# Layer norm folded into the next product of a two-layer decoder step

## The chip, the cores and the metric

The kernel runs on one core of a Trainium2 chip. The time is the device time of one execution in microseconds (us). Three executions were timed, and their median is the time before. The times of instructions come from one more execution, taken with the hardware profiler.

The engines of the core are named TensorE (PE in the profile, its weight loads PEld), VectorE (DVE), ScalarE (ACT), GpSimd (POOL) and SyncE (SP). Each works through its own queue in order. They wait for each other with semaphores.

## The reference

264 tokens (256 of a prompt, 8 of running samples) with 2048 features go through two layers. Each layer is a mixer and an MLP, and each of the four steps ends in a layer norm of a residual sum:

```python
def layer_norm(x, g, b):
    mu = jnp.mean(xf, axis=-1, keepdims=True)
    var = jnp.mean(jnp.square(xf - mu), axis=-1, keepdims=True)
    y = (xf - mu) * lax.rsqrt(var + LN_EPS)
    return y * g + b
...
x = layer_norm(ALPHA * x + mixer(x))
x = layer_norm(ALPHA * x + jnp.square(jax.nn.relu(x @ w1)) @ w2)
```

The first layer's mixer is a sparse attention beside a convolution, the second's a pooling beside a gated MLP ("odd" in the code). Both have one input projection and one output projection. The MLP has 8192 hidden features. All is float32, and the matmuls must come close to float32.

## The kernel before

**Products.** Features lie on partitions, tokens on columns: `x`, `yacc` and `sq` are 128 x 16 x 264, with 16 tiles k of 128 features. All large products are cut into 89 weight groups `G` of 512 output features (4 banks of `psa`) by 2048 input features: 0 to 9 the first input projection, 10 to 13 its output projection (`G_EOUT`), 14 to 45 the first MLP, 46 to 52 the odd input projection (`G_OIN`), 53 to 56 the odd output projection, 57 to 88 the second MLP. An MLP is four rounds of eight groups: four "hidden" groups that give 2048 hidden features, and four "product" groups that add to `yacc`.

**Split in two.** Every product is made of three: the weights are split into `whi` (rounded to the matmul's format) and `wlo` (the rest), the input likewise into `xhi` and `xlo` (`hhi` and `hlo` for the hidden features), and L414 to L416 do high x high, high x low and low x high. A group has four pieces `p` of 4 tiles k, each with 4 banks, and so 192 matmuls of 264 columns. `split(G, p)` stands in two queues: on ScalarE (L946) it makes `whi` once the buffer is free, on VectorE (L1320) it then makes `wlo`. There are two buffers, so the split of piece 0 of the next group waits for piece 2 of this one, that of piece 1 for the end of this group, that of piece 2 for piece 0 of its own group, and that of piece 3 for piece 1. TensorE waits with `lo_ready` for each piece. The weights come by DMA a whole group ahead.

**Order.** The queues are written out by hand. In a hidden group (`hidden`), ScalarE's queue holds the splits of pieces 2 and 3 of this group (`later`), that of piece 0 of the next, then for each bank a Relu out of `psa` (L1233, which frees the bank) and the high part `hhi` of the square (L1238), and near the end the split of piece 1 of the next group. VectorE's queue holds the same splits, then the squares (L1835) and the low parts (L1838). In the first round ScalarE also makes the residual ALPHA * x (L1179).

**The norm.** `last_groups` (VectorE) and `norm` (ScalarE, TensorE) close each of the four steps. VectorE adds the product groups to `yacc` and sums them over k. In the last group it subtracts a preliminary mean of the first 12 tiles (L1765, after one matmul with ones, L843), ScalarE squares, and after the last bank TensorE sums over partitions with four matmuls with ones (L849 to L854). VectorE then makes mean, variance and inverse root, centres and divides `yacc` in five chunks (L1815, L1816), ScalarE applies gain and bias to give `x` (L1213) and its high part `xhi` (L1217), and VectorE the low part (L1811), which lets TensorE start the next group piece by piece. `L` counts the norms, 0 to 3; 0 to 2 are followed by a product, 3 by the output.

**The odd projection.** ScalarE evicts its groups straight from `psa`: group 46 into `pext` and `psx`, with a wait for all seven small loads of this layer (`odd_in`), the others through Gelu (L1277, L1287).

Of the kernel before, what the change touches and what calls it, by code (L numbers as in the profile page):

```python
# [25 lines left out]
D = 2048  # L26
# [46 lines left out]
ln_sum ln_mean ln_cent ln_sq ln_var ln_tot ln_part ln_norm ln_x ln_xhi y_init  # L73
# [4 lines left out]
win_out odd_in pin_done u_done gelu_v vtr vcopied vn_done wst_done mix_mm mix_ev pool_d pool_mm sgs_tr sgs_done  # L78
# [4 lines left out]
def build(nc, io):  # L83
    with ExitStack() as ctx:
# [32 lines left out]
        xhi = new("xhi", [128, KT, NT], F32R)  # L117
        xlo = new("xlo", [128, KT, NT], F32R)
# [45 lines left out]
        b = Region(region_b, region_a)  # L164
# [92 lines left out]
        def _(sp):  # L257
# [68 lines left out]
            for i in range(4):  # L326
                sp.wait_ge(s.ln_x, 3 * KT + 4 * i + 4)
                sp.dma_start(io.o_x[:, 4 * i * NT:(4 * i + 4) * NT], x[:, 4 * i:4 * i + 4, :].rearrange("p k t -> p (k t)"))\
                    .then_inc(s.x_out, 16)
# [4 lines left out]
        def _(pool):  # L334
# [43 lines left out]
            pool.dma_start(psx[:].rearrange("p c b w -> p (c b w)"), io.stpool).then_inc(s.odd_in, 16)  # L378
# [6 lines left out]
            pool.wait_ge(s.bank_free, 4 * (G_OIN + 1))  # L385
# [10 lines left out]
        def _(pe):  # L396
            mm = nc.tensor.matmul

            def group(G, hi, lo, xbase=None, hooks=None):

                nt = tiles(G)
                for p in range(4):
# [3 lines left out]
                    for n in range(nt):  # L406
                        if p == 0 and not (isinstance(G, int) and G == 0):
                            pe.wait_ge(s.bank_free, 4 * G - 3 + n)
                        for kk in range(4):
# [3 lines left out]
                            out = psa[:, n, 0:NT]  # L413
                            mm(out, wh, hi[:, k, :], start=(k == 0), stop=False)  # L414
                            mm(out, wh, lo[:, k, :], start=False, stop=False)  # L415
                            last = mm(out, wl, hi[:, k, :], start=False, stop=(k == KT - 1))  # L416
# [421 lines left out]
            def mean_hook(L):  # L838

                def hook(p, n):  # L840
                    if p == 0 and n == 3:
                        pe.wait_ge(s.ln_sum, L + 1)
                        mm(psm[:, 0, 0:NT], ones, s1[:], start=True, stop=True).then_inc(s.ln_mean, 1)  # L843
                return hook

            def norm(L):

                pe.wait_ge(s.ln_part, L + 1)
                mm(psm[:, 0, 0:NT], ones, s1[:], start=True, stop=False)  # L849
                mm(psm[:, 1, 0:NT], ones, s2[:], start=True, stop=False)  # L850
                pe.wait_ge(s.bank_free, 4 * (G_MLP0, G_OIN, G_MLP1, G_END)[L])
                mm(psm[:, 0, 0:NT], ones, yacc[:, KT - 1, :], start=False, stop=True)
                pe.wait_ge(s.ln_sq, 7 * L + 7)
                mm(psm[:, 1, 0:NT], ones, sq[:, KT - 1, :], start=False, stop=True).then_inc(s.ln_tot, 1)  # L854

            def mlp(G0, L, xbase, hbase):
                with pe.Fori(0, 3) as f:
                    with pe.Fori(0, 4) as g:
                        group(G0 + f * 8 + g, xhi, xlo, (s.x_ready, xbase))
# [3 lines left out]
                with pe.Fori(0, 4) as g:  # L863
                    group(G0 + 24 + g, xhi, xlo)
                group(G0 + 28, hhi, hlo, (s.hid_ready, hbase + 48))
                with pe.Fori(5, 7) as g:
# [1222 lines left out]
```

## Time and profile before

| | |
|---|---|
| median of 3 runs | 2646.7 us |
| lowest and highest | 2639.17 and 2647.37 us |
| the profiled execution | 2640.75 us |
| its span, first to last instruction | 2639.1 us |
| granted TensorE clock over the span | 0.944 of full |
| TensorE busy, matmuls | 2441.2 us, 93% |
| VectorE busy | 1472.7 us, 56% |
| ScalarE busy | 991.0 us, 38% |
| DMA | 516 MB, 196 GB/s |

A difference of two times is set against the profiled execution's own time. The share of busy time says how much an engine works over the whole span, and not whether its work is in time: an engine that is half idle can hold up another one, if what the other one wants stands late in its queue. A wait is put down to the operation that ended last before it. The granted clock is the share of its full 2.4 GHz at which TensorE was let run; 0.50 is 1.2 GHz.

### The profile page before, as it was taken

The page shows a single profiled execution, that of the slowest core. Times are in us where ns is not written, and L with a number is a line of the kernel's source. Part 1 is how long each engine was busy: PE and PEld are TensorE (multiplying, and loading weights), DVE is VectorE, ACT ScalarE, POOL GpSimd, SP SyncE. Part 2 cuts the span into 40 slices and gives each one's busy share as a digit, 9 for nine tenths or more (in the row PEclk, how much of TensorE's full clock was granted, in tenths as well). Part 3 has the DMA queues.
Part 4 walks back from the last instruction along what each step waited for, and adds up shares of the span by engine and source line. Part 5 has one row for each costly group of instructions (what it writes and reads, how often), then busy time and mean ns, then how long its engine had stood idle before and what let it go on. Part 6 is the DMA issues. An engine that isn't in the chain of part 4 may idle for free.

```text
span 2639.1 us, 51324 instructions
## 1 busy us (share of the span) xinstructions
PE 2441.2 (93%) x20534; PEld 2279.2 (86%) x20534; DVE 1472.7 (56%) x1695; ACT 991.0 (38%) x1117; POOL 87.0 (3%) x169
## 2 busy tenths in 40 slices
PE   4999998888979999999999799679899999999996
PEld 3778871577979999999999799569799999999996
DVE  3677777556665454445455644666654544444556
ACT  2233330344354344343343444233543443443433
POOL 0000013230000000000000000000000000000000
PEclk8999995888989999999999899879899999999998
DMA  7788779787535555555544354324355455455451
GB/s 284 256 311 311 267 196 267 249 262 262 177 136 200 209 199 203 186 204 200 208 181 176 128 203 175 128 77 176 113 182 183 175 182 183 175 182 184 175 182 75
DMA packets 99715, 515.98 MB, mean 196 GB/s; under 512 B 12824, under 2 KB 21048, under 8 KB 52512
## 3 DMA queue, kind: packets, MB, share of 16 engines
q1 hardware_dynamic: 88992, 467.90, 50.2%
q0 software_dynamic: 10624, 46.72, 5.4%
q8 instruction: 67, 1.10, 0.2%
q14 instruction: 32, 0.26, 0.0%
HBM read 508.17 MB, written 18.95 MB: 200 GB/s over the span
## 4 chain that ended last, share of the span: by engine, by line
PE 83%; DVE 8%; DMA 3%; ACT 2%; issue 2%; SPq 0%; POOL 0%; POOLq 0%; ACTq 0%; DVEq 0%
PE psa L414 25%; PE psa L415 24%; PE psa L416 24%; DVE wlo L1320 2%; DMA page<-in_cmp 2%; PE psa L577 2%; PE psm L450 1%; ACT whi L946 1%; PE psm L770 1%; PE psa L749 1%; DMA kbuf<-in_selk 1%; DVE yacc L1815 1%; PE psm L602 1%; DVE page L1336 1%; PE psa L602 1%
## 5 line engine op out<-in xcount | busy, mean ns | idle before, releaser
L1320 DVE TENSOR_TENSOR wlo<-wraw,whi 128x2048 fp32r<-128x2048 f32 x356 | 816.2, 2293 | 934.6 <-ACT whi L946 934.4
L414 PE MATMUL psa<-xhi,whi 128*128 128x264 f32 x3632 | 1050.4, 289 | 57.8 <-DVE xlo L1811 23.3
L946 ACT ACTIVATE whi<-wraw 128x2048 fp32r<-128x2048 f32 x356 | 681.5, 1914 | 1116.3 <-PE psa L416 1114.9
L415 PE MATMUL psa<-xlo,whi 128*128 128x264 f32 x3632 | 1041.0, 287 | 0.0
L416 PE MATMUL psa<-xhi,wlo 128*128 128x264 f32 x3632 | 1036.3, 285 | 0.0
L414 PEld LDWEIGHTS psa<-xhi,whi 128*128 128x128 f32 x3632 | 692.4, 191 | 95.0 <-issue 84.4
L415 PEld LDWEIGHTS psa<-xlo,whi 128*128 128x128 f32 x3632 | 692.5, 191 | 0.1
L416 PEld LDWEIGHTS psa<-xhi,wlo 128*128 128x128 f32 x3632 | 690.9, 190 | 0.0
L414 PE MATMUL psa<-hhi,whi 128*128 128x264 f32 x2048 | 582.6, 284 | 0.0
L415 PE MATMUL psa<-hlo,whi 128*128 128x264 f32 x2048 | 582.1, 284 | 0.0
L416 PE MATMUL psa<-hhi,wlo 128*128 128x264 f32 x2048 | 580.1, 283 | 0.0
L414 PEld LDWEIGHTS psa<-hhi,whi 128*128 128x128 f32 x2048 | 385.4, 188 | 0.1
L415 PEld LDWEIGHTS psa<-hlo,whi 128*128 128x128 f32 x2048 | 385.4, 188 | 0.1
L416 PEld LDWEIGHTS psa<-hhi,wlo 128*128 128x128 f32 x2048 | 384.8, 188 | 0.0
L1336 DVE TENSOR_TENSOR page<-page,pe_rep 128x768 f32<-128x768 f32 x128 | 115.8, 953 | 18.1 <-DMA page<-in_cmp 17.5
L450 PE MATMUL psm<-page,const 128*32 128x384 f32 x512 | 57.2, 520 | 23.3 <-DVE page L1336 23.3
L577 PE MATMUL psa<-kbuf,qzr 96*32 96x512 f32 x320 | 64.6, 903 | 13.2 <-DMA kbuf<-in_selk 13.1
L1238 ACT ACTIVATE hhi<-stage 128x264 f32 x128 | 53.5, 418 | 45.0 <-DVE stage L1835 45.0
L1116 ACT ACTIVATE pp<-pp,hg 128x128 f32<-128x128 f32 (+1 forms) x64 | 28.4, 445 | 108.9 <-DVE hg L1607 108.9
L1732 DVE TENSOR_TENSOR yacc<-psa,yacc 128x264 f32 (+1 forms) x144 | 55.4, 427 | 23.8 <-PE psa L416 23.8
L1838 DVE TENSOR_TENSOR hlo<-stage,hhi 128x264 f32 x128 | 55.1, 430 | 13.4 <-ACT hhi L1238 12.2
L1233 ACT ACTIVATE stage<-psa 128x264 f32<-128x264 f32 x128 | 48.9, 382 | 27.0 <-PE psa L416 23.4
(351 smaller groups left out, 1214.2 us busy)
## 6 DMA issues: line engine op xcount, KB each, us to landing
wraw<-in_w SPq DMA_DIRECT2D x356, 1024.0 KB, 4.8
page<-in_cmp SPq DMA_DIRECT2D x128, 384.0 KB, 4.8
kbuf<-in_selk SPq DMA_DIRECT2D x64, 192.0 KB, 5.5
kbuf<-in_selk POOLq DMA_DIRECT2D x64, 192.0 KB, 5.6
vbuf<-in_selv SPq DMA_DIRECT2D x64, 192.0 KB, 3.9
vbuf<-in_selv POOLq DMA_DIRECT2D x64, 192.0 KB, 4.0
o_win<-in_win POOLq DMA_DIRECT2D x8, 1533.0 KB, 7.7
kbuf<-in_wink SPq DMA_DIRECT2D x8, 768.0 KB, 6.6
```

Source lines behind the costliest of these rows:

```text
L414: mm(out, wh, hi[:, k, :], start=(k == 0), stop=False)
L415: mm(out, wh, lo[:, k, :], start=False, stop=False)
L416: last = mm(out, wl, hi[:, k, :], start=False, stop=(k == KT - 1))
L450: last = mm(psm[c:c + 32, 2, 0:KW], C("blkz", 28 - 4 * r, 60 - 4 * r), page[:, (2 * r + q) % 8, half * KW:half * KW + KW], start=(r == 0), ...
L577: last = mm(psa[32 * g:32 * g + 32, c % 2, :], qzr[:, r, 32 * g:32 * g + 32], kbuf[:, u % 4, :, g * 128:(g + 1) * 128], start=(r == 0), st ...
L602: last = mm(bank[32 * g:32 * g + 32, d:d + HD], p_t, vbuf[:, u % 5, q, g * HD:(g + 1) * HD], start=(q == 0 and c == 0), stop=(q == 3 and ( ...
L946: A(whi[:, p % 2, :], wraw[:, p, :], ACT.Copy).then_inc(s.hi_ready, 1)
L1238: A(hhi[:, bass.ds(4 * g + n - 1, 1), :], stage[:, n - 1:n, :], ACT.Copy).then_inc(s.hh_done, 1)
L1320: V.tensor_tensor(wlo[:, p % 2, :], wraw[:, p, :], whi[:, p % 2, :].bitcast(F32), ALU.subtract).then_inc(s.lo_ready, 1)
L1336: V.tensor_tensor(v, v, bc(pe_rep[:].rearrange("p a (g d) -> p a g d", g=1), 128, 2, KVH, HD), ALU.mult)\
L1732: V.tensor_tensor(y, psa[:, n:n + 1, 0:NT], y, ALU.add).then_inc(s.bank_free, 1)
L1838: V.tensor_tensor(hlo[:, bass.ds(4 * g + n - 1, 1), :], stage[:, n - 1:n, :], hhi[:, bass.ds(4 * g + n - 1, 1), :].bitcast(F32), ALU.subtr ...
```

## The change

The norms 0 to 2 no longer stand between the sum and the next product. The product is taken of the centred sum z times the gain g, not divided by the root. With W the weights, r the inverse root and m the remaining mean of z over the features, the next layer's input is r (z - m) g + b, so

(input @ W) = r ((z g) @ W - m (g @ W)) + b @ W.

- `xhi` and `xlo` get two more columns, 264 and 265, with g and b of the features. The groups that follow a norm (32 hidden and 7 odd ones) so have matmuls of 266 columns, and the last two columns of each bank hold g @ W and b @ W.
- `fold` takes the place of `last_groups` and `norm` for norms 0 to 2. The preliminary mean is that of the first 8 tiles and comes one group earlier (TensorE's `shift_hook`, in the third of the last four groups). All four parts of `yacc` are centred in that group. In the last group the high and low parts of z g are made, and the squares. The sums over partitions are two matmuls with ones (`total_hook`) inside piece 1 of the next product's first group. The root (`spread_root`) lies in that group between the splits of pieces 2 and 3.
- The eviction moves from ScalarE to VectorE: `evict` copies the two columns into `gb`, adds m times g @ W (a `scalar_tensor_tensor` out of `psa`, which frees the bank), and multiplies by r, all three for each bank. ScalarE's Relu or Gelu reads that and adds b @ W as its bias.
- The normalised x itself is still needed, for the residual sum. `whole` makes it in the first four groups after each of these norms: two VectorE operations over 1056 columns and four ScalarE operations for each group. In the MLPs they write `yacc`, already times ALPHA (`alph`).
- The small loads of the odd layer: `psx` has its own semaphore, and the six others are issued after x is complete and awaited later.
- Norm 3 keeps the old form (`final_groups`).

```diff
-                            out = psa[:, n, 0:NT]
-                            mm(out, wh, hi[:, k, :], start=(k == 0), stop=False)
+                            out = psa[:, n, 0:w]
+                            mm(out, wh, hi[:, k, 0:w], start=(k == 0), stop=False)
...
+            def total_hook(L):
+
+                def hook(p, n):
+                    if p == 1 and n == 1:
+                        pe.wait_ge(s.z_part, L + 1)
+                        mm(psm[:, 0, 0:NT], ones, s1[:], start=True, stop=True)
+                        mm(psm[:, 1, 0:NT], ones, s2[:], start=True, stop=True).then_inc(s.z_tot, 1)
+                return hook
...
ScalarE
+            def whole(L, i, dst, done):
+
+                act.wait_ge(s.z_norm, 4 * L + i + 1)
+                for k in range(4 * i, 4 * i + 4):
+                    ins = A(dst[:, k, :], yacc[:, k, :], ACT.Identity, scale=alph[:, 32 * L + k:32 * L + k + 1],
+                            bias=alph[:, 32 * L + 16 + k:32 * L + 17 + k])
...
+            def hidden(G, g, m, hb, first=None):
+
+                if first is not None and first[1] == 0:
+                    spread_root(first[0], G)
+                else:
                     later(G)
+                split(G + 1, 0)
+                for n in range(5):
+                    if n == 3:
+                        split(G + 1, 1)
+                    if n < 4:
+                        act.wait_ge(s.ev_done, hb + (28 if hb > 64 else 0) + 4 * m + n)
+                        A(stage[:, n, :], stage[:, n, :], ACT.Relu, bias=gb[:, n, 1:2]).then_inc(s.relu_done, 1)
+                    if n >= 1:
+                        act.wait_ge(s.sq_done, hb - 1 + 4 * m + n)
+                        A(hhi[:, bass.ds(4 * g + n - 1, 1), :], stage[:, n - 1:n, :], ACT.Copy).then_inc(s.hh_done, 1)
+                if first is not None:
+                    whole(first[0], first[1], yacc, s.y_init)
...
VectorE
+            def spread_root(L, Gn):
+
+                split(Gn, 2)
+                dve.wait_ge(s.z_tot, L + 1)
+                step(V.tensor_scalar(mean[:], psm[:, 0, 0:NT], -1.0 / D, None, ALU.mult))
...
+                inverse_root(V.tensor_scalar(rstd[:], rstd[:], EPS, None, ALU.add), rstd[:])
+                split(Gn, 3)
+
+            def evict(G, n, count):
+
+                dve.wait_ge(s.bank_done, 4 * G + n + 1)
+                V.tensor_copy(gb[:, n, :], psa[:, n, NT:NT + 2]).then_inc(s.gb_done, 1)
+                dve.wait_ge(s.gb_done, count)
+                V.scalar_tensor_tensor(stage[:, n, :], mean[:], gb[:, n, 0:1], psa[:, n, 0:NT], ALU.mult, ALU.add).then_inc(s.bank_free, 1)
+                dve.wait_ge(s.bank_free, 4 * G + n + 1)
+                V.tensor_tensor(stage[:, n, :], stage[:, n, :], rstd[:], ALU.mult).then_inc(s.ev_done, 1)
+
+            def whole(L, i):
+
+                v = yacc[:, 4 * i:4 * i + 4, :]
+                step(V.tensor_tensor(v, v, along(mean, 4), ALU.add))
+                V.tensor_tensor(v, v, along(rstd, 4), ALU.mult).then_inc(s.z_norm, 1)
...
+            def hidden(G, g, m, hb, first=None):
...
+                split(G + 1, 0)
+                dve.wait_ge(s.hid_ready, hb + 4 * m)
+                for n in range(6):
+                    if n == 4:
                         split(G + 1, 1)
+                    if n < 4:
+                        evict(G, n, hb + (28 if hb > 64 else 0) + 4 * m + n)
+                    if 1 <= n < 5:
+                        dve.wait_ge(s.relu_done, hb - 1 + 4 * m + n)
+                        V.tensor_tensor(stage[:, n - 1, :], stage[:, n - 1, :], stage[:, n - 1, :], ALU.mult).then_inc(s.sq_done, 1)
+                    if n >= 2:
+                        dve.wait_ge(s.hh_done, hb - 2 + 4 * m + n)
+                        V.tensor_tensor(hlo[:, bass.ds(4 * g + n - 2, 1), :], stage[:, n - 2:n - 1, :],
+                                        hhi[:, bass.ds(4 * g + n - 2, 1), :].bitcast(F32), ALU.subtract).then_inc(s.hid_ready, 1)
+                if first is not None:
+                    whole(*first)
```

The groups of the odd projection run the same way with Gelu and without squares: ScalarE has its split of piece 1 ahead of the fourth Gelu, VectorE behind the four evictions, and `whole` closes the first four groups in both queues.

## Rows read from the trace of the kernel before

**Rows 1.** The page, busy time, share of the span and instructions of each engine.

```profile
PE 2441.2 (93%) x20534; PEld 2279.2 (86%) x20534; DVE 1472.7 (56%) x1695; ACT 991.0 (38%) x1117; POOL 87.0 (3%) x169
```

**Rows 2.** Waits of TensorE over the span: line, releaser, us in total, times, longest.

```profile
PE psa L414 <- DVE xlo L1811: 23.3, 2, 11.7
PE psa L414 <- DVE wlo L1320: 21.2, 4, 17.4
PE psm L849 <- DVE s L1790: 18.9, 4, 5.4
PE psa L414 <- issue: 11.5, 1, 11.5
```

**Rows 3.** Windows between norms: length, busy us (x instructions) of each engine, clock, DMA.

```profile
900.00:950.00 50.00, 50.00 (x415) 50.00 (x414) 23.55 (x17) 15.75 (x9) 0.49 (x1) 1.00 0.55 209
```

**Rows 4.** Timeline of ScalarE, splits at two norms: start, duration, instruction, [idle <- releaser].

```profile
703.90 1.92 ACT L946 ACTIVATE whi<-wraw 128x2048 fp32r<-128x2048 f32 x1 [3.94 <-PE psa L416]
...
710.19 1.92 ACT L946 ACTIVATE whi<-wraw 128x2048 fp32r<-128x2048 f32 x1 [4.38 <-PE psa L416]
...
776.19 1.92 ACT L946 ACTIVATE whi<-wraw 128x2048 fp32r<-128x2048 f32 x1 [2.90 <-PE psa L416]
...
1475.05 1.92 ACT L946 ACTIVATE whi<-wraw 128x2048 fp32r<-128x2048 f32 x1 [3.94 <-PE psa L416]
...
1550.89 1.92 ACT L946 ACTIVATE whi<-wraw 128x2048 fp32r<-128x2048 f32 x1 [3.57 <-PE psa L416]
```

**Rows 5.** Timeline of VectorE in a hidden group of the first MLP.

```profile
978.34 0.77 DVE L1835 TENSOR_TENSOR stage<-stage 128x264 f32<-128x264 f32 x2
...
982.67 2.29 DVE L1320 TENSOR_TENSOR wlo<-wraw,whi 128x2048 fp32r<-128x2048 f32 x1 [1.24 <-ACT whi L946]
```

**Rows 6.** Timeline of ScalarE in the same group.

```profile
980.74 1.90 ACT L946 ACTIVATE whi<-wraw 128x2048 fp32r<-128x2048 f32 x1
...
985.83 1.92 ACT L946 ACTIVATE whi<-wraw 128x2048 fp32r<-128x2048 f32 x1 [2.88 <-PE psa L416]
```

**Rows 7.** Groups of VectorE by form: busy us, mean ns of one, idle before.

```profile
L1626 DVE TENSOR_TENSOR hg<-hg,gt 128x2 f32<-128x2 f32 x16 | 2.6, 161 | 0.6
L1518 DVE SCALAR_TENSOR_TENSOR stage<-uext,param,stage 128x256 f32<-128x256 f32 x120 | 50.9, 480 | 0.9
L1835 DVE TENSOR_TENSOR stage<-stage 128x264 f32<-128x264 f32 x128 | 52.0, 427 | 0.0
L1816 DVE TENSOR_TENSOR yacc<-yacc,rstd 128x1056 f32<-128x1056 f32 x12 | 15.1, 1259 | 1.3
```

**Rows 8.** Groups of ScalarE by form, the same columns.

```profile
L1238 ACT ACTIVATE hhi<-stage 128x264 f32 x128 | 53.5, 418 | 45.0 <-DVE stage L1835 45.0
L1213 ACT ACTIVATE x<-yacc,param 128x264 f32<-128x264 f32 x64 | 34.1, 597 | 23.3 <-DVE yacc L1816 23.3
```

**Rows 9.** Timelines: gaps of TensorE, restarts after a waited split, four x operations.

```profile
530.96 0.45 PE L624 MATMUL psm<-const,tok 128*96 128x128 f32 x1 [3.00 <-ACT ptp L1067]
...
741.91 2.11 ACT L1213 ACTIVATE x<-yacc,param 128x264 f32<-128x264 f32 x4 [1.65 <-DVE yacc L1816]
...
1543.25 0.39 PE L414 MATMUL psa<-xhi,whi 128*128 128x264 f32 x1 [1.74 <-ACT psx L1269]
...
1876.14 2.29 DVE L1320 TENSOR_TENSOR wlo<-wraw,whi 128x2048 fp32r<-128x2048 f32 x1 [0.48 <-ACT whi L946]
...
1878.48 0.39 PE L414 MATMUL psa<-xhi,whi 128*128 128x264 f32 x1 [1.41 <-DVE wlo L1320]
...
1884.58 1.92 ACT L946 ACTIVATE whi<-wraw 128x2048 fp32r<-128x2048 f32 x1 [4.58 <-PE psa L416]
```

**Rows 10.** Windows after such gaps, the columns of rows 3.

```profile
1513.70:1519.70 6.00, 5.96 (x27) 5.99 (x28) 5.89 (x5) 3.84 (x7) 0.00 (x0) 0.50 0.39 146
1543.80:1547.20 3.40, 3.40 (x18) 3.40 (x17) 1.15 (x1) 3.38 (x6) 1.27 (x2) 0.50 0.61 212
...
531.00:535.00 4.00, 4.00 (x43) 3.35 (x44) 0.00 (x0) 0.98 (x2) 0.29 (x2) 0.50 0.70 253
```

More of the change, by code:

```diff
@@ L116, in build @@
         region_b = new.next
-        xhi = new("xhi", [128, KT, NT], F32R)
-        xlo = new("xlo", [128, KT, NT], F32R)
+        xhi = new("xhi", [128, KT, NT + 2], F32R)
+        xlo = new("xlo", [128, KT, NT + 2], F32R)
+        alph = new("alph", [128, 128])
+        gb = new("gb", [128, 4, 2])
         region_a = new.next
@@ L924, in _ @@
             group(G_OOUT, xhi, xlo, (s.x_ready, 64))
-            with pe.Fori(G_OOUT + 1, G_OOUT + 3) as G:
-                group(G, xhi, xlo)
-            group(G_OOUT + 3, xhi, xlo, None, mean_hook(2))
-            norm(2)
+            group(G_OOUT + 1, xhi, xlo)
+            group(G_OOUT + 2, xhi, xlo, None, shift_hook(2))
+            group(G_OOUT + 3, xhi, xlo)
             mlp(G_MLP1, 3, 80, 65)
@@ L1185, in first_groups @@
                 for i in range(4):
-                    residual(i)
+                    residual(i, x, scale)
                 split(G0 + 1, 0)
                 split(G0 + 1, 1)
-                with act.Fori(G0 + 1, G0 + 3) as G:
-                    later(G)
-                    split(G + 1, 0)
-                    split(G + 1, 1)
-            first_groups(G_EOUT, 8)
-            def norm(L):
-                G = (G_MLP0, G_OIN, G_MLP1, G_END)[L] - 1
+                later(G0 + 1)
+                split(G0 + 2, 0)
@@ L1219, in hidden @@
[L1219 to L1238 removed]
+                        act.wait_ge(s.ln_norm, k0 + m)
@@ new lines, in hidden @@
+            def hidden(G, g, m, hb, first=None):
+                if first is not None and first[1] == 0:
+                    spread_root(first[0], G)
+                else:
+                    later(G)
+                split(G + 1, 0)
+                dve.wait_ge(s.hid_ready, hb + 4 * m)
+                for n in range(6):
+                    if n == 4:
+                        split(G + 1, 1)
+                    if n < 4:
[9 more added lines that the diff above has]
+                    whole(*first)
@@ L1841, in mlp, with products @@
             def mlp(G0, L, hb, y):
-                with dve.Fori(0, 3) as f:
-                    hidden(G0, f, hb)
+                def products(f):
                     dve.wait_ge(s.y_init, 4 * y)
```

430 lines of the change are left out of this document (263 added, 167 removed).

## The prediction, made blind

> **What bounds the kernel now.** I read the page first. TensorE is busy 93% of the span and VectorE 56% [rows 1]: the kernel is a chain of weight groups on TensorE, and the question is which waits interrupt it. The waits of TensorE give the norms: it waits for the last square sum and then for the first normalised piece of the next input, 17.1 us at each of the three inner norms (two of the long ones stand under `xlo`, the third under "issue") [rows 2]. The stretches come next: between norms TensorE is busy all 50.00 of 50 us, 415 matmuls at 120.5 ns, full clock, so nothing waits there [rows 3]. A group of 192 matmuls takes 23.3 us (the value that the split times below repeat) and a piece (a quarter) 5.83.
>
> What a norm costs in all is read from ScalarE's splits. The split of piece 2 starts when TensorE has finished piece 0 of the same group. From the last group before the norm (703.90) to the second after it (776.19) are 72.3 us, at the second norm 75.8, at the third 72.3 again (its rows repeat the first's) [rows 4]. Two undisturbed groups are 46.6, so the norms cost 25.7 + 29.2 + 25.7 = 80.6 us beyond plain groups. In them lie the waits, five small fp32 products with ones, and half clock after the idle time: from 1513.7 the granted clock is 0.50 and 27 matmuls take 6 us, 220 ns each; at full clock they would take 3.2 [rows 10].
>
> **What the change removes.** The next product starts on centred, unscaled data, so its pieces are ready before the norm's sums are, and TensorE waits for neither. I work out what remains at each inner norm. The four adds of the last group come behind a weight split and the `low` operations on VectorE, bank 0 is freed some 0.5 us late, with a restart 0.8. Two fp32 ones products inside the next group: 0.9 (one such product lengthens a piece from 5.83 to 6.29, as 703.90 to 710.19 shows for the mean product; I use 0.46 for each) [rows 4]. Root and reciprocal lie between two splits on VectorE and make pieces 2 and 3 a few tenths late each, with restarts 0.9. The mean product is moved a group earlier and not removed, 0.46. Sum 3.1, three times 9.2. Saved: 80.6 - 9.2 = **71.4 us**. The 3.6 us more of the second norm are in it: its evictions waited for the small odd-layer loads, which the change takes off ScalarE's wait. The last norm stays as it is.
>
> **The two columns.** 39 groups (32 of the two MLPs, 7 of the odd projection) x 192 matmuls get 266 columns for 264. In proportion to 120.5 ns that is 0.91 ns each, **6.8 us**. The lower bound is nothing: 264 columns take 220 ns at half clock, so 110 at full, and 120.5 is seen [rows 3, 10]; if what adds the 10.5 is not additive, the columns hide in it. I take the upper end. The Trainium skill ("TensorE: Matmul & The Clock Gate", Back-to-back issue gap) gives N/2.4 + 2.5 ns at full clock for a lone stream; this trace is 8 ns above that, and by the page two columns would be 0.83 ns, 6.2 us in all.
>
> **The eviction, the part that I think decides.** Before, ScalarE evicts a bank in one Relu. After, VectorE makes copy, multiply-add, multiply before ScalarE's Relu, then squares. The busy share says that VectorE has room (9 us in each group). The order in its queue says otherwise, because the split of piece 1 of the next group stands behind all of this, and it can't be made earlier: ScalarE's half waits for the end of the group. Take the hidden group that ends at 980.0. Before: ScalarE's half 980.74, VectorE's half 982.67 to 984.96; TensorE finishes piece 0 at 985.83 and needs it then. The spare time is 0.87 us [rows 5, 6].
>
> Now the new order, from 978.34, where VectorE leaves the preceding split [rows 5]. Durations: copy of two columns 0.17 (a two-column operation takes 0.161), multiply-add with a scalar operand 0.49 (0.480 on 256 columns), products and subtractions 0.43 [rows 7]; a dependent one follows 0.04 after the end, an independent one 0.08 before it, as the neighbours in the timeline show. Relu with a bias operand 0.54: a copy takes 0.42 and one with scale and bias 0.60 [rows 8]. Bank 0: copy 978.34, multiply-add 978.55, multiply to 979.51. Bank 1: copy 979.44, multiply to 980.61, square 0 to 980.96. Bank 2: copy 980.89, multiply to 982.06, square 1 to 982.41, low part 0 to 982.76. Bank 3: copy 982.69, multiply to 983.86, square 2, low part 1 to 984.56. ScalarE meanwhile: Relu 2 at 982.08, high part 1 to 982.97, and behind them, by its order, the split, 982.90 to 984.81. VectorE's half then runs 984.83 to 987.12, **2.16 us later than before**. TensorE stands idle for 1.3 us. A piece that starts on a waited split ends 6.14 us after the split (1878.43 to 1884.57) and not 5.83 [rows 9], so piece 1 ends at 993.3 and not 991.7: **1.6 us** a group. The banks themselves are free in time (bank 3 at 983.4, wanted at 984.4). Of the 32 hidden groups 24 are of this form: 38.4 us.
>
> On the small operations the Trainium skill ("VectorE: DVE Perf Modes", The TRN2 errata) says that each one pays a fixed latency, 120 cycles at 0.96 GHz from PSUM, and that many small tiles pay it each time; that speaks against this eviction, and its estimate for the two-column copy is 0.13 us. By it the chain would be 0.04 shorter for each bank and the sum 5 us lower.
>
> **The whole x, kept for the residual.** In the first four groups of each MLP VectorE's queue ends with square 3 and low parts 2 and 3 (to 988.38), then add and multiply over 1056 columns, 1.25 each [rows 7], to 990.86; ScalarE must wait for that, makes four with scale and bias in 2.11 [rows 9], to 992.99, and only behind them comes the split of piece 2, to 994.84, and VectorE's half to 997.15. Piece 1 was done at 993.3: idle 3.9 us, and piece 2 ends at 1003.3 for 999.1, **4.2 more**. 8 groups x (1.6 + 4.2) = 46.4 us. The residual that ScalarE made there before lay in its free time and gives nothing back.
>
> The odd projection has no squares. The same count puts the split of piece 1 at 986.42 (0.9 lost) and of piece 2 at 995.19 (idle 2.7, 2.9 lost): 4 groups x 3.8 + 2 x 0.9 = 17.0 us.
>
> **The clock after the new gaps.** After 1.74 us of idle (ended 1543.25) the next matmuls went 220 ns apart at a granted clock of 0.50, 18 of them, 1.8 us lost; after 3.00 (ended 530.96) it was 0.50; after 11.5 the loss was 2.8. After 1.41 (ended 1878.48) and the like the pace stayed full [rows 9, 10]. So I charge the 12 gaps of 2.7 to 3.9 us with 2.2 each, **26 us** (bounds 22 and 34), and the gaps of 1.3 with nothing (upper bound 1.8 for each of about 32, 58 us).
>
> **Sum**, against the profiled execution's own 2640.75 us (its span 2639.1; 6 below the median of 2646.7): -71.4 + 6.8 + 38.4 + 46.4 + 17.0 + 26 = +63.2, so **2704 us**, 2.4% slower.
>
> **Rivals.**
> (a) *The new gaps arise but the clock holds.* 2640.75 + 37 = 2678. For it: three gaps of 1.2 to 1.4 us left no trace. Against: the gap of 1.74.
> (b) *The gaps of 1.3 us lower the clock too.* 2704 plus 20 to 58, say 2735. They are just below the 1.74 that did it, and come in every group. The Trainium skill ("TensorE: Matmul & The Clock Gate", A second HAM failure mode) tells of a kernel that idled briefly between groups and kept oscillating between both clocks.
> (c) *Faster: the splits keep up.* The place is the split of piece 1 behind the evictions: up to a delay of 0.87 us it costs nothing, and I count 2.16. If the operations were some 0.3 us shorter for each bank than their rows, and the whole x fitted into the same free time, no gap would be left: 2640.75 - 71.4 + 6.8 = 2576. For it speaks only the free time by the busy shares.
> (d) *Half of it:* piece 1 keeps up and only the whole x is late: 8 x 4.2 + 4 x 2.9 = 45, clock 0 to 26: 2621 to 2647, about the same time.
>
> **How the numbers follow.** Forecast 0.50, (a) 0.20, (b) 0.13, (c) 0.08, (d) 0.09. A measurement of this kernel can tell about 0.3% (8 us) from no change. Faster: (c) and over half of (d), 0.13. Same: 0.05. Slower: 0.82. The range takes in (a) with operations 0.1 us shorter for each bank (some 20 us less over all groups) and most of (b): 2655 to 2748.
>
> **What would show it.** The timeline of a hidden group: the split of piece 1 ends 7.1 us after the group's end, TensorE waits some 1.3 us for `wlo`; in the first four groups of an MLP a second wait of about 3.9 us. Group period 24.9 and some 29 to 31 against 23.3. The waits for `wlo` (21.2 now) become by far the largest, some 90 us more; those for `xlo` and `s` vanish but for the last norm. The granted clock falls in the first groups of each MLP. The prediction is wrong if `wlo` stays near 21, or if ScalarE's split of piece 1 doesn't wait behind the Relus.

## The result, and the profile of the changed kernel

The changed kernel takes 2698.8 us (median of 4 runs, 2694.1 to 2704.5), the kernel before 2647.0 beside it (4 runs, 2639.2 to 2655.0): ratio 1.0193, 95% interval 1.0165 to 1.0221, so slower by 1.9%. The profiled execution took 2695.44 us with a span of 2693.7; that of before took 2640.75 with 2639.1. The two spans differ by 54.6 us, and this is the sum that is taken apart below.

The page's busy times, which answer to [rows 1], and the chain that ended last:

```profile
PE 2474.0 (92%) x20522; PEld 2306.7 (86%) x20522; DVE 1628.4 (60%) x2194; ACT 1003.6 (37%) x1140; POOL 86.9 (3%) x169
...
PE 68%; DVE 15%; ACT 9%; issue 5%; DMA 2%; SPq 0%; DVEq 0%; ACTq 0%; POOLq 0%; POOL 0%
```

VectorE does 156 us more work in 499 more instructions and still is busy for only 60% of the span. By that line alone nothing is wrong. The waits of TensorE (line, releaser, us in total, times, longest) say where it went:

```profile
PE psa L417 <- DVE wlo L1394: 94.8, 49, 17.5
...
PE psm L868 <- DVE s L1956: 2.6, 1, 2.6
PE psa L417 <- DVE yacc L1877: 1.7, 3, 0.6
```

Against [rows 2] the waits for `xlo` are gone and those for `s` have shrunk from 18.9 to 2.6. What is left of the three inner norms is 1.7 us in three waits of 0.5 to 0.6 for the last adds (L1877), which free the banks; the prediction had 0.5 each. In their place stands the low half of the weights: 94.8 us in 49 waits, where it was 21.2 in 4. These are the new gaps. In the first MLP, from the norm to the fifth group, and then in a later hidden group, TensorE's timeline (start, duration, instruction, [idle before <- releaser]) has them as follows:

```profile
758.70 0.39 PE L417 MATMUL psa<-xhi,whi 128*128 128x266 f32 x1 [1.34 <-DVE wlo L1394]
...
768.69 0.41 PE L417 MATMUL psa<-xhi,whi 128*128 128x266 f32 x1 [3.79 <-DVE wlo L1394]
...
789.30 0.39 PE L417 MATMUL psa<-xhi,whi 128*128 128x266 f32 x1 [1.06 <-DVE wlo L1394]
...
799.30 0.39 PE L417 MATMUL psa<-xhi,whi 128*128 128x266 f32 x1 [3.79 <-DVE wlo L1394]
...
999.55 0.39 PE L417 MATMUL psa<-xhi,whi 128*128 128x266 f32 x1 [1.05 <-DVE wlo L1394]
```

Two kinds of gap: one of about 1.05 us before piece 1 of the group that follows each hidden group, and one of 3.8 before piece 2 of the group that follows each of the first four. Why there is a gap before piece 1 stands in the timelines of VectorE and of ScalarE around the group that ends at 992.6 (the gap at 999.55 begins at 998.50, and one piece before that is 992.6). They answer to [rows 5, 6]:

```profile
993.30 0.15 DVE L1903 COPY gb<-psa 128x2 f32<-128x2 f32 x1
993.49 0.49 DVE L1905 SCALAR_TENSOR_TENSOR stage<-mean,gb,psa 128x264 f32<-128x264 f32 x1
994.02 0.43 DVE L1907 TENSOR_TENSOR stage<-stage,rstd 128x264 f32<-128x264 f32 x1
994.37 0.43 DVE L1994 TENSOR_TENSOR stage<-stage 128x264 f32<-128x264 f32 x1
994.71 0.43 DVE L1997 TENSOR_TENSOR hlo<-stage,hhi 128x264 f32 x1
995.06 0.15 DVE L1903 COPY gb<-psa 128x2 f32<-128x2 f32 x1
...
997.20 2.29 DVE L1394 TENSOR_TENSOR wlo<-wraw,whi 128x2048 fp32r<-128x2048 f32 x1 [0.32 <-ACT whi L974]
```

```profile
994.93 0.42 ACT L1309 ACTIVATE hhi<-stage 128x264 f32 x1
995.26 1.91 ACT L974 ACTIVATE whi<-wraw 128x2048 fp32r<-128x2048 f32 x1
...
1000.48 1.92 ACT L974 ACTIVATE whi<-wraw 128x2048 fp32r<-128x2048 f32 x1
...
1025.49 1.92 ACT L974 ACTIVATE whi<-wraw 128x2048 fp32r<-128x2048 f32 x1
```

VectorE works on the banks without a pause, operation after operation. ScalarE splits piece 1 only at 995.26, behind three Relus and two high parts that each wait for VectorE, and VectorE's half ends at 999.49. TensorE wanted it at 998.50. The split of piece 2 begins at 1000.48 and that of the next group at 1025.49, 25.0 us later; in the kernel before the corresponding ones, 962.54 and the 985.83 of [rows 6], are 23.29 apart.

The second kind comes from the whole x. VectorE's and ScalarE's timelines behind the third hidden group:

```profile
821.02 1.25 DVE L1912 TENSOR_TENSOR yacc<-yacc,mean 128x1056 f32<-128x1056 f32 x1
822.31 1.26 DVE L1913 TENSOR_TENSOR yacc<-yacc,rstd 128x1056 f32<-128x1056 f32 x1
827.54 4.50 DVE L1394 TENSOR_TENSOR wlo<-wraw,whi 128x2048 fp32r<-128x2048 f32 x2 [3.97 <-ACT whi L974]
```

```profile
823.60 2.10 ACT L1271 ACTIVATE yacc<-yacc,alph 128x264 f32<-128x264 f32 x4 [2.96 <-DVE yacc L1913]
825.61 3.70 ACT L974 ACTIVATE whi<-wraw 128x2048 fp32r<-128x2048 f32 x2
```

Two operations on VectorE, then four on ScalarE, then the split. VectorE itself is idle for 3.97 us ahead of its half, waiting for ScalarE's, which waited for VectorE: an engine with idle time in front of the very work that is late.

The windows of TensorE (length, busy us (x instructions) of PE, PEld, DVE, ACT, POOL, granted clock, DMA share, GB/s): 50 us of later hidden groups, and the stretch behind two of the long gaps.

```profile
955.00:1005.00 50.00, 47.90 (x386) 47.47 (x386) 31.97 (x48) 21.93 (x24) 0.49 (x1) 1.00 0.55 200
...
768.70:772.00 3.30, 3.30 (x15) 3.30 (x16) 2.14 (x1) 0.00 (x0) 0.00 (x0) 0.53 0.59 199
799.30:803.00 3.70, 3.70 (x18) 3.70 (x19) 2.15 (x1) 0.00 (x0) 0.00 (x0) 0.55 0.66 226
```

With gaps of 1.05 us in it the first window still has the full clock. Behind the gaps of 3.8 us the clock is at half: 18 matmuls in 3.70 us, which at 121.3 ns each would take 2.18, so 1.5 us are lost.

**By stretches.** I cut both traces at ScalarE's split of piece 2, as the prediction did. From the last group before the first norm to the sixth after it, before takes 165.5 us and after 171.4; over the same groups of the last norm of this kind 165.5 and 171.8; at the odd norm 169.1 and 158.9. The first four groups after each MLP norm take 30.6 (before 23.3), the first four odd groups 27.2, so the norms themselves got cheaper by 23.5 (5.9 more, of which 4 x 7.3 are these groups), 25.8 (10.2 less, in spite of 4 x 3.9) and 23.1 us, 72.4 in all. The 26 groups that follow in each MLP, of which 12 are hidden groups at 25.0, take 627.3 and 626.9 for 605.7: 21.7 and 21.2 more. The rest of the 54.6 lies in the input projection and the attention stage (3.4), in the odd layer's own mixer (4.0, with one wait in it that grew by 3.9: TensorE waits 4.4 us for the last Gelu where it waited 0.5), and in 1.2 us each at two stretches that I had not looked for: the plain output projection groups in them, with matmuls of 264 columns as before and no new operation, take 23.55 us each for 23.29.

### The profile page after: what moved, and what is told of

The parts are those of the page before. It is cut to its first block, busy times and chain, and to the rows that moved or that the text cites. A ratio compares the mean times of both kernels' runs of the same rounds, so it can differ in the third digit from the quotient of the medians.

```text
span 2693.7 us, 51259 instructions
## 1 busy us (share of the span) xinstructions
PE 2474.0 (92%) x20522; PEld 2306.7 (86%) x20522; DVE 1628.4 (60%) x2194; ACT 1003.6 (37%) x1140; POOL 86.9 (3%) x169
## 4 chain that ended last, share of the span: by engine, by line
PE 68%; DVE 15%; ACT 9%; issue 5%; DMA 2%; SPq 0%; DVEq 0%; ACTq 0%; POOLq 0%; POOL 0%
PE psa L417 20%; PE psa L418 19%; PE psa L419 19%; ACT whi L974 7%; DVE wlo L1394 5%; DVE stage L1905 2%; PE psa L580 2%; PE psm L453 2%; PE psm L773 1%; DMA kbuf<-in_selk 1%; DVE stage L1907 1%; PE psa L752 1%; DVE stage L1994 1%; DMA page<-in_cmp 1%; DVE yacc L1913 1%
## 5 line engine op out<-in xcount | busy, mean ns | idle before, releaser
L417 PE MATMUL psa<-xhi,whi 128*128 128x266 f32 (+1 forms) x3632 | 1060.0, 292 | 79.3 <-DVE wlo L1394 77.6
L418 PE MATMUL psa<-xlo,whi 128*128 128x266 f32 (+1 forms) x3632 | 1048.4, 289 | 0.0
L419 PE MATMUL psa<-xhi,wlo 128*128 128x266 f32 (+1 forms) x3632 | 1046.7, 288 | 0.0
L417 PEld LDWEIGHTS psa<-hhi,whi 128*128 128x128 f32 x2048 | 386.7, 189 | 19.3 <-DVE wlo L1394 13.6
L1306 ACT ACTIVATE stage<-stage,gb 128x264 f32<-128x264 f32 x128 | 65.5, 512 | 144.3 <-DVE stage L1907 144.3
L1905 DVE SCALAR_TENSOR_TENSOR stage<-mean,gb,psa 128x264 f32<-128x264 f32 x156 | 76.4, 490 | 5.5
L1309 ACT ACTIVATE hhi<-stage 128x264 f32 (+1 forms) x128 | 53.7, 419 | 65.9 <-DVE stage L1994 65.9
L1907 DVE TENSOR_TENSOR stage<-stage,rstd 128x264 f32<-128x264 f32 x156 | 67.5, 433 | 5.3
```

What stands on the lines that cost most here:

```text
L417: mm(out, wh, hi[:, k, 0:w], start=(k == 0), stop=False)
L418: mm(out, wh, lo[:, k, 0:w], start=False, stop=False)
L419: last = mm(out, wl, hi[:, k, 0:w], start=False, stop=(k == KT - 1))
L1306: A(stage[:, n, :], stage[:, n, :], ACT.Relu, bias=gb[:, n, 1:2]).then_inc(s.relu_done, 1)
L1905: V.scalar_tensor_tensor(stage[:, n, :], mean[:], gb[:, n, 0:1], psa[:, n, 0:NT], ALU.mult, ALU.add).then_inc(s.bank_free, 1)
L1907: V.tensor_tensor(stage[:, n, :], stage[:, n, :], rstd[:], ALU.mult).then_inc(s.ev_done, 1)
```

## The experiments

Three things are open. Does the place of the split in the queues decide, or the amount of VectorE's work? Do the short gaps cost clock? And what slows groups that do nothing new? (The texts written before the runs call runs 1, 2 and 3 e1, e2 and e3, the two of run 4 e7 and e8, run 5 e4, the three of run 6 e5, e6 and e9, and run 7 e10.)

**1. Evict first.** The same instructions as the changed kernel in another order. VectorE makes the four evictions and square 0, then its half of the split, then the other squares and the low parts; ScalarE has its half behind the first Relu (the odd groups: behind the first Gelu instead of the third).

```diff
ScalarE
-                for n in range(5):
-                    if n == 3:
-                        split(G + 1, 1)
...
+                relu(0)
+                split(G + 1, 1)
+                high(0)
+                for n in range(1, 4):
+                    relu(n)
+                for n in range(1, 4):
+                    high(n)
VectorE
-                for n in range(6):
-                    if n == 4:
-                        split(G + 1, 1)
...
+                for n in range(4):
+                    evict(G, n, hb + (28 if hb > 64 else 0) + 4 * m + n)
+                    if n == 1:
+                        square(0)
+                split(G + 1, 1)
+                for n in range(1, 4):
+                    square(n)
...
```

(`relu`, `high` and `square` are the operations of one bank with their waits, taken out of the old loop; the four low parts follow.)

> Edit: the changed kernel with its queues in another order and the same instructions. VectorE makes all four evictions (square 0 among them), then its half of the split of piece 1, then the rest; ScalarE makes its half behind the first Relu or Gelu. The whole x stays where it is. My theory (what costs is the place of the split of piece 1 in the two queues): the 24 later hidden groups go from 25.0 to about 23.6 us each, the first four of each MLP gain little (the whole x then costs 4.9 where it cost 4.2, so some 0.6 each), the odd groups 0.5: about -40 us, 2659. Rival (the added work of VectorE itself costs, wherever it stands): no change from the changed kernel, 2699.

Measured: 2669.3 us, ratio to before 1.0059 (1.0039 to 1.0080); 29.5 less than the changed kernel, 10 more than expected. The mechanism came as foreseen: the later hidden groups take 23.70 us for 25.0, with no gap. The first groups did not gain: they still take 30.4 to 30.9, because the squares and low parts now stand between the split and the whole x, so that its gap grew to 4.5 to 4.8 us, by about what the other had lost. TensorE's rows and the windows behind the gap:

```profile
780.29 0.59 PE L417 MATMUL psa<-xhi,whi 128*128 128x266 f32 x1 [4.80 <-DVE wlo L1399]
...
871.77 0.59 PE L417 MATMUL psa<-hhi,whi 128*128 128x264 f32 x1 [4.72 <-DVE wlo L1399]
```

```profile
780.30:784.80 4.50, 4.50 (x21) 4.50 (x22) 2.13 (x1) 0.00 (x0) 0.00 (x0) 0.54 0.71 266
871.80:876.00 4.20, 4.20 (x19) 4.20 (x20) 2.11 (x1) 0.00 (x0) 0.00 (x0) 0.50 0.78 261
```

After 4.8 us idle the clock is at half for about 4 us (21 matmuls in 4.50 us, which at 121.3 ns would take 2.55, so 2.0 are lost).
In the odd groups the gap before piece 2 shrank from 2.52 to 1.8 us, and still two of the three group times stayed at 27.3 us (27.2 in the changed kernel), for the clock now fell after three of the four gaps:

```profile
1559.42 0.39 PE L417 MATMUL psa<-xhi,whi 128*128 128x266 f32 x1 [1.79 <-DVE wlo L1399]
...
1585.18 0.39 PE L417 MATMUL psa<-xhi,whi 128*128 128x266 f32 x1 [1.79 <-DVE wlo L1399]
```

```profile
1559.40:1563.40 4.00, 3.98 (x32) 3.98 (x33) 2.29 (x1) 0.24 (x1) 0.00 (x0) 1.00 0.65 233
1585.20:1590.20 5.00, 5.00 (x28) 5.00 (x29) 2.29 (x1) 0.20 (x1) 0.00 (x0) 0.66 0.80 275
```

The same gap twice, once at full clock (25.8 us for the group) and once not (27.3).

The attention stage ahead of all this took 301 us in the profile of this run, for 288 in the changed kernel's. It holds none of the change, and those 13.6 us are more than the 10 by which the run missed its expectation. Over the twelve profiles this stage took 285 to 292 us in eight and 299 to 304 in four; why is open, and it is the main doubt in comparing single profiles.

**2. The whole x late.** Of the changed kernel only the place of `whole` is another: on VectorE between the splits of pieces 2 and 3 of the next group, on ScalarE behind both. The evictions stay as they are.

```diff
 VectorE, hidden
-                    later(G)
+                    split(G, 2)
+                    whole(first[0], first[1] - 1)
+                    split(G, 3)
...
-                if first is not None:
-                    whole(*first)
 ScalarE, hidden
                     later(G)
+                    if first is not None:
+                        whole(first[0], first[1] - 1, yacc, s.y_init)
```

> Edit: the changed kernel, only the whole x moved. VectorE makes it in the next group between the splits of pieces 2 and 3, ScalarE behind both splits; same instructions. My theory (ScalarE's split of piece 2 stands behind x): the first four groups of each MLP go from 30.6 to 25.0 us each, the first odd groups from 27.2 to 24.3, the granted clock no longer falls in them: about -57 us, 2642. The 24 later hidden groups stay at 25.0. Rival (the added work of VectorE itself costs): no change, 2699.

Measured: 2639.3 us, ratio 0.9976 (0.9961 to 0.9991), 59.5 less than the changed kernel and as expected within 3 us. The first MLP groups take 25.03 us for 30.6, the odd ones 24.37 for 27.18, the later ones stay at 25.0. This run also settles the clock. Its hidden groups all have the gap of 1.05 to 1.3 us, 32 in all, and the window over two of them, and the waits, are:

```profile
955.00:1005.00 50.00, 47.91 (x387) 47.48 (x386) 31.95 (x48) 21.92 (x24) 0.49 (x1) 1.00 0.54 199
```

```profile
PE psa L417 <- DVE wlo L1397: 54.3, 37, 17.7
```

The granted clock is 1.00 through both MLPs. So the short gaps cost no clock (a group loses 1.3 us, the gap of 1.05 and the restart), and rival (b) falls.

**3. Both orders.** Edits 1 and 2 together; the same operations as in the changed kernel.

```diff
VectorE, hidden
-                    later(G)
+                    split(G, 2)
+                    whole(first[0], first[1] - 1)
+                    split(G, 3)
...
+                for n in range(4):
+                    evict(G, n, hb + (28 if hb > 64 else 0) + 4 * m + n)
+                    if n == 1:
+                        square(0)
+                split(G + 1, 1)
```

> Edit: both orders at once, same instructions as the changed kernel. My theory: no wait of TensorE for wlo above the ones of the kernel before, all hidden and odd groups at 23.6 to 23.7 us, full clock: about -103 us from the changed kernel, 2596, and so some 50 us (1.9%) under the kernel before. Rival (VectorE's added work costs by itself): 2699; half of it: 2645, as before.

Measured: 2592.5 us, ratio 0.9785 (0.9767 to 0.9802), 106 us less than the changed kernel and 2.1% faster than the kernel before. The page, the wait for the weights, VectorE's rows around a hidden group and the window:

```profile
PE 2446.5 (94%) x20522; PEld 2288.7 (88%) x20522; DVE 1623.5 (63%) x2194; ACT 999.2 (39%) x1140; POOL 87.2 (3%) x169
```

```profile
PE psa L417 <- DVE wlo L1402: 17.7, 1, 17.7
```

```profile
987.16 0.15 DVE L1911 COPY gb<-psa 128x2 f32<-128x2 f32 x1
...
990.70 0.15 DVE L1911 COPY gb<-psa 128x2 f32<-128x2 f32 x1
990.89 0.49 DVE L1913 SCALAR_TENSOR_TENSOR stage<-mean,gb,psa 128x264 f32<-128x264 f32 x1
991.41 0.43 DVE L1915 TENSOR_TENSOR stage<-stage,rstd 128x264 f32<-128x264 f32 x1
991.76 2.29 DVE L1402 TENSOR_TENSOR wlo<-wraw,whi 128x2048 fp32r<-128x2048 f32 x1
```

```profile
955.00:1005.00 50.00, 50.00 (x407) 50.00 (x407) 33.85 (x49) 21.94 (x25) 0.49 (x1) 1.00 0.59 215
```

VectorE has 2194 instructions and 1623.5 us of work, as in the changed kernel (2194, 1628.4), and the one wait for the weights that is left is that for the very first ones, at the start of the kernel. The four evictions, with square 0 among them, take 4.6 us in a row, the split ends at 994.05, and TensorE needs it 0.77 us later. All 32 hidden and 7 odd groups run without such a gap, 23.70 us from one to the next. The added work on VectorE costs TensorE nothing in this order, so what the changed kernel loses to its gaps it loses by the order.

**4. Another copy.** A second copy of the two columns for each bank, once in the changed kernel and once in run 3, one execution each. If the queue decides, it costs in the first and nothing in the second.

```diff
+        gb = new("gb", [128, 8, 2])
...
+                V.tensor_copy(gb[:, 4 + n, :], psa[:, n, NT:NT + 2])
                 V.tensor_copy(gb[:, n, :], psa[:, n, NT:NT + 2]).then_inc(s.gb_done, 1)
```

> Edit: the changed kernel with a second two-column copy for each bank on VectorE, the result unused. Theory (VectorE's chain up to the split of piece 1 sets the period of a hidden group): each of the four copies adds its 0.07 to 0.15 us in full, the later hidden groups go from 25.01 to between 25.3 and 25.6. Rival (TensorE's gap comes from elsewhere): 25.01 stays.

> Edit: both orders as in e3 with the same second copy for each bank. Theory: in this order the split of piece 1 has 0.77 us to spare and the four copies take 0.3 to 0.6, so the same added work costs nothing here: hidden groups stay at 23.70 us. Rival (the work of VectorE costs by itself): 24.0 to 24.3, as much more as in e7.

Measured: 2715.3 and 2593.8 us; in the first the attention stage took 299 us for 288, so the totals are no measure here and the groups are. The later hidden groups went from 25.01 to 25.21 in the changed kernel and stayed at 23.70 in run 3, with the waits for the weights:

```profile
PE psa L417 <- DVE wlo L1394: 101.9, 51, 17.5
```

```profile
PE psa L417 <- DVE wlo L1402: 17.5, 1, 17.5
```

The first waits 7.1 us longer in all than without the copy, the second not. The copy lengthens a group by 0.20 us, 0.05 for each bank and not its 0.15, for the two copies of a bank overlap, as VectorE's timeline in the first shows:

```profile
1002.61 0.15 DVE L1903 COPY gb<-psa 128x2 f32<-128x2 f32 x1
1002.68 0.15 DVE L1904 COPY gb<-psa 128x2 f32<-128x2 f32 x1
```

My range for the first was 25.3 to 25.6, so the direction holds and the size was too high. A side effect that I had not asked for: the product groups went from 23.31 to 23.39 in both, though nothing was done to them but that the larger `gb` moved `hhi` by 32 bytes.

**5. The layout alone.** In the kernel before, `xhi` and `xlo` get the 266 columns of the changed kernel; 264 are written and read as ever. There is no fold, no new operation.

```diff
-        xhi = new("xhi", [128, KT, NT], F32R)
-        xlo = new("xlo", [128, KT, NT], F32R)
+        xhi = new("xhi", [128, KT, NT + 2], F32R)
+        xlo = new("xlo", [128, KT, NT + 2], F32R)
...
-                            mm(out, wh, hi[:, k, :], start=(k == 0), stop=False)
+                            mm(out, wh, hi[:, k, 0:NT], start=(k == 0), stop=False)
```

> Edit: the kernel before, only xhi and xlo laid out with 266 columns for each tile k (1064 bytes for 1056), of which 264 are read, as before. In the changed kernel the groups that read 264 of 266 columns take 23.55 us where they took 23.29. Theory (the layout costs 1.3 ns a matmul): all 57 groups that read xhi and xlo take 0.26 us longer, +15 us, 2662. Rival (the 0.26 comes from the other work beside the matmuls): no change, 2647.

Measured: 2658.8 us, ratio 1.0046 (1.0028 to 1.0065). ScalarE's splits of piece 2 in two neighbouring groups:

```profile
969.72 1.92 ACT L946 ACTIVATE whi<-wraw 128x2048 fp32r<-128x2048 f32 x1 [2.99 <-PE psa L416]
...
993.27 1.92 ACT L946 ACTIVATE whi<-wraw 128x2048 fp32r<-128x2048 f32 x1 [3.00 <-PE psa L416]
```

23.55 us, where the same two groups of before stand at 962.54 and 985.83, 23.29 apart; the groups that read `hhi`, whose layout is the old one, stay at 23.29. So 0.26 us in each of the 57 groups that read x come from where the rows of x lie (their pitch, or the start of `xlo`, which moves with it; the run doesn't tell them apart), and 192 matmuls are paced 1.35 ns wider. The sum, 15 us, is in the measured 12 and its interval (7 to 17).

**6. Other layouts.** I took it that the pitch of a feature tile in bytes should be a multiple of 32, as 1056 is and 1064 isn't. So run 3 with 272 columns (1088 bytes), before with 268 (1072 bytes; one execution), and run 3 with 268.

```diff
-        xhi = new("xhi", [128, KT, NT + 2], F32R)
-        xlo = new("xlo", [128, KT, NT + 2], F32R)
+        xhi = new("xhi", [128, KT, NT + 8], F32R)
+        xlo = new("xlo", [128, KT, NT + 8], F32R)
```

> Edit: both orders as in e3, and xhi and xlo laid out with 272 columns for each tile k (1088 bytes, a multiple of 32 as 1056 is and 1064 isn't); 266 or 264 of them are read. Theory (what costs 0.26 us a group is the start of each tile k off a multiple of 32 bytes): all 57 groups that read xhi and xlo get 0.26 shorter, a 264-column one 23.29 again, a 266-column one 23.44: -15 us from e3, 2578. Rival (any layout wider than what is read costs): 2592, 23.55 and 23.70 stay.

> Edit: the kernel before with xhi and xlo laid out with 268 columns (1072 bytes, a multiple of 16 but not of 32), 264 read. If a multiple of 16 is enough, the groups that read xhi and xlo take 23.29 us as before; if it must be 32, 23.55 or between.

> Edit: both orders as in e3, xhi and xlo laid out with 268 columns. e6 showed 23.34 us for a 264-column group in that layout, e4 and e5 23.55 to 23.57 with 266 and 272. If the layout acts the same here, the 57 groups that read xhi and xlo get 0.2 us shorter: hidden groups 23.5 for 23.70, -12 us from e3, 2581. Rival (e6's 23.34 belongs to the kernel before alone, by where its other tiles lie): 23.70 and 2592 stay.

Measured: 2594.0 us (0.9781, 0.9749 to 0.9813), 2657.4, and 2598.2 (0.9795, 0.9770 to 0.9819). The two of run 3 were expected at 2578 and 2581 and gained nothing. The 2657.4 of before with 268 columns stands beside a median of 2652.5 for the kernel before, and its attention stage took 304 us for 286, so the time says nothing of the layout there. By group, in us:

```
bytes from tile to tile    264 columns read    266 columns read
1056                       23.29               -
1064                       23.55               23.70
1072                       23.32 to 23.34      23.79
1088                       23.57 (*)           23.84
```

(*) This is the figure of the first layer's output projection in run 3 with 272 columns; the like groups of the odd layer's output projection took 23.25 in the same run. So with 1088 bytes even groups of one kind differ, and with 1072 the 264-column groups are nearly as fast as ever and the 266-column ones slower. Neither a multiple of 32 nor of 16 explains this, and no rule that I tried does. The effect is shown; its cause stays open.

**7. The loads of the odd layer.** Before, with `psx` on a semaphore of its own, so that ScalarE does not await the other six small loads (one execution).

```diff
-            pool.dma_start(psx[:].rearrange("p c b w -> p (c b w)"), io.stpool).then_inc(s.odd_in, 16)
+            pool.dma_start(psx[:].rearrange("p c b w -> p (c b w)"), io.stpool).then_inc(s.pool_in, 16)
...
-            act.wait_ge(s.odd_in, 16 * 7)
+            act.wait_ge(s.pool_in, 16)
```

> Edit: the kernel before, in which ScalarE's evictions of the first odd group wait for the load of psx alone and VectorE waits for the six others later. My count: the stretch over the second inner norm falls from 75.8 to 72.3 us, 3.5 of the 71.4 us saved by the change. Rival (the loads' wait was hidden, the 3.5 come from something else): it stays at 75.8.

Measured: 2636.8 us, span 2635.1 for 2639.1. The splits at the second norm:

```profile
1474.63 1.92 ACT L946 ACTIVATE whi<-wraw 128x2048 fp32r<-128x2048 f32 x1 [3.94 <-PE psa L416]
...
1546.93 1.92 ACT L946 ACTIVATE whi<-wraw 128x2048 fp32r<-128x2048 f32 x1 [2.24 <-PE psa L416]
```

72.3 us apart, where [rows 4] have 75.8 there and 72.3 at the two other norms. The 3.5 us are the loads', and they need no folding of the norm to be had.

## Why the prediction was right, and where it was not

The time (2699 for 2704), the direction and the mechanism came as forecast. But the sum was +63 for +55 in the profile, and two of its larger errors offset each other, so that the time came this close is in part luck. Term by term, in us over the whole kernel:

```
term                               predicted   measured   from
norms                              -71.4       -72.4      stretches over the three norms
two more columns, 39 groups        +6.8        +5.9       23.70 against 23.55: 0.15 a group
gap before piece 1, 24 groups      +38.4       +31.2      25.0 against 23.70
both gaps, first 8 MLP groups      +46.4       +43.6      30.6 - 23.70 - 1.45 of clock
odd groups                         +17.0       +14.0      27.18 against 23.70, four groups
clock                              +26         +12.7      8 x 1.45 and once 1.1
layout of x, 57 groups             0           +14.8      23.55 against 23.29
mixer stages and the rest          0           +5
sum                                +63.2       +54.6
```

**The norms.** The step "sum 3.1, three times 9.2" held within a us a norm, the loads of the odd layer within it (run 7: 3.5 us of the predicted 3.6).

**The two columns.** Of the bounds 0 and 0.91 ns a matmul, the upper was taken; 0.15 us over 192 matmuls are 0.8 ns. The columns do not hide in the 10.5 ns that the prediction left unexplained. The formula of the Trainium skill ("TensorE: Matmul & The Clock Gate", Back-to-back issue gap) gives an estimate of 0.83 for them, and this trace agrees, though the formula's constant of 2.5 ns is 9 short here (121.3 ns for 264 columns). The 120.5 that the prediction worked with was 0.8 low (192 matmuls in 23.29 us make 121.3), which changes nothing here.

**The eviction.** This was the step that decided, and it can be laid beside the trace. Predicted from the group's end: bank 3's copy at 2.69 us, ScalarE's split at 2.90, VectorE's end of the split at 7.12. Measured, with the end at 992.6: 2.5, 2.7 and 6.9 (copy at 995.06, split at 995.26, end at 999.49). The 0.24 us by which all of it is earlier are the operations, each a little below its row: copy 0.15 for 0.17, and Relu with a bias 0.51 for 0.54, as these groups (busy us, mean ns of one | idle before) show:

```profile
L1306 ACT ACTIVATE stage<-stage,gb 128x264 f32<-128x264 f32 x128 | 65.5, 512 | 144.3 <-DVE stage L1907 144.3
L1905 DVE SCALAR_TENSOR_TENSOR stage<-mean,gb,psa 128x264 f32<-128x264 f32 x156 | 76.4, 490 | 5.5
...
L1907 DVE TENSOR_TENSOR stage<-stage,rstd 128x264 f32<-128x264 f32 x156 | 67.5, 433 | 5.3
```

The gap is so 1.05 for 1.3, and a group loses 1.30 for 1.6. On the copy the Trainium skill ("VectorE: DVE Perf Modes", The TRN2 errata) gave an estimate of 0.13, which was on the other side of the measured 0.15. Rival (c) wanted the operations 0.3 us shorter for each bank; they were about 0.06 shorter. Its time, 2576, is however near what the same operations reach in the order of run 3, 2592: I had the free time right, and the rival should have been put as a question of order.

**The whole x.** 3.79 us for 3.9 before piece 2. The operations came with the durations of their rows ([rows 7]: 1.26 each; [rows 9]: four in 2.11), and the estimate is within 0.1 us.

**The odd groups.** The gap before piece 2 is 2.52 for 2.7. The gap before piece 1 came in these four groups only, 0.59 us once and 0.40 three times; the last two odd groups lost nothing, where 0.9 each was charged.

**The clock.** This is the term that was mis-sized. "So I charge the 12 gaps of 2.7 to 3.9 us with 2.2 each": after the eight of 3.8 to 3.9 us the clock fell each time, but the loss is about 1.5 (15 matmuls in 3.30 us, 18 in 3.70). After the four odd gaps, all of 2.52 us, it fell only once. The windows behind the third and the fourth:

```profile
1619.60:1623.60 4.00, 4.00 (x32) 4.00 (x33) 2.14 (x1) 0.00 (x0) 0.00 (x0) 1.00 0.64 236
1646.80:1650.80 4.00, 4.00 (x23) 4.00 (x24) 2.08 (x1) 0.00 (x0) 0.53 (x1) 0.65 0.98 324
```

The same gap, once at full clock and once at half for its first 2 us. I had taken 2.2 as a middle between 1.8 (a gap of 1.74) and 2.8 (one of 11.5). The 1.8 was itself read too high: behind that gap the matmuls of the kernel before start 216 to 220 ns apart 15 times and 174 once, which makes 1.5 us, as much as after 3.8. Nor does the length of a gap decide alone: of the five gaps of 1.74 to 1.82 us in all runs four lowered the clock (the one of the kernel before and three of run 1's four), and of the nine of 2.41 to 2.53 also four. The gaps of about 1 us, charged with nothing, cost no clock. The oscillation that the Trainium skill tells of ("TensorE: Matmul & The Clock Gate", A second HAM failure mode), which stood behind rival (b), does not show itself here at 1.05 us of idle in each 25.

**The layout of x.** This step was missing. "Adds two columns" was costed by what is streamed, and not by what else moves when an array gets a new pitch. Its 15 us offset the 13 by which the clock was charged too high: with the layout alone put right the forecast would have been 2719, with the clock alone 2691, both in the range and both farther from 2699 than it is.

**The rivals.** (a), the clock holds, was true in three of the four odd gaps and in none of the eight others; the bare time is 21 us off. (b) falls with run 2. (c) and (d) did not come by the operations being shorter, but their conditions can be made: run 3 is (c), and run 1 is (d), where piece 1 keeps up and the whole x is late. It took 2669 and not 2621 to 2647, since its gap before piece 2 is 4.5 to 4.8 us and not 3.9, by the layout's 15 us, and by its slow attention stage.

## What to carry to other kernels

Where an engine has work with a due time and work without one in the same queue, cost a change by that queue's order in one period and not by its busy share: here the same instructions took 106 us more in one order than in another, on an engine that was busy for 60% and 63%. If operations must be added, put the piece that the bottleneck waits for behind only what frees the next one's buffers, and everything else behind it, in the stretch that is idle today. And when an operand's array grows by a column, measure the new layout alone, without the change.

## What the runs showed of the hardware

- The pace of a stream of matmuls depends on where its moving operand lies, at the same number of columns: 121.3 ns with 1056 bytes from tile to tile, 122.7 with 1064 (run 5), and 121.8 for 121.4 when an array moves by 32 bytes (run 4). Which property of the address it is was not found.
- Ahead of the large products of all runs TensorE's clock stayed at full (1.00) after each of 108 idle times of 1.04 to 1.72 us, and was at half behind each of 37 of 3.0 us and more, the wait at the start of the kernel aside. Between them the length did not decide: it fell after four of five of 1.74 to 1.82 us and after four of nine of 2.41 to 2.53. After 3.8 us idle it lost 1.5 us, after 4.8 us 2.0.
- A small operation right behind a like one on VectorE costs 0.05 us, not the 0.15 that it takes by itself (run 4).
- A ScalarE operation over 264 columns takes 0.09 us more with a bias pointer (a Relu 0.512 and a Gelu 0.51, for 0.418 of a copy), with scale and bias together 0.18 (0.597, [rows 8]).
